# Feed-forward heads: the row of roots, the first copy of low sums and the order of the first two tiles

## The reference, cut to what matters

```
def conv_ffn(h, w_up, dw_w, dw_b, w_down):
    u = dwconv(h @ w_up, dw_w, dw_b)            # 3 taps along the tokens
    val, gate = jnp.split(u, 2, axis=-1)
    return (jax.nn.gelu(gate) * val) @ w_down
...
    h = rmsnorm(x, norm2_g[i])                  # a row of 256 inverse roots, one per token
    x = x + conv_ffn(h, ffn_w_up[i], ffn_dw_w[i], ffn_dw_b[i], ffn_w_down[i])
```

## Time and profile before

| | us |
|---|---|
| median of 3 runs (1609.86 to 1610.27) | 1610.09 |
| the profiled execution's own time | 1610.04 |
| span from its first to its last instruction | 1608.1 |
| PE busy in the span | 1573.2 (98%) |
| DVE busy | 1248.2 (78%) |
| ACT busy | 996.0 (62%) |
| DMA, mean rate over the span | 177 GB/s |

### The profile page before, as it was taken

One profiled execution on the slowest core, in us unless ns is written; L12 is line 12 of the kernel. 1 busy time (PEld: TensorE's weight loads), 2 busy tenths in 40 slices (PEclk: granted clock), 3 DMA queues, 4 the chain that ended last, 5 costly groups with the idle time before them and its releaser, 6 DMA issues.

```text
span 1608.1 us, 25361 instructions
## 1 busy us (share of the span) xinstructions
PE 1573.2 (98%) x8810; PEld 1344.2 (84%) x8810; DVE 1248.2 (78%) x1828; ACT 996.0 (62%) x1406; POOL 102.4 (6%) x110
## 2 busy tenths in 40 slices
PE   9999999999999999999999999999999999999998
PEld 9887888878878889868888898868788887878887
DVE  6756888878798887866888886456788887878887
ACT  6576665675676656666666655444666666666664
POOL 0031000000000001340000042000100000000000
PEclk9999999999999999999999999999999999999999
DMA  9434455543645554443555555524555554345553
GB/s 344 153 111 171 181 188 203 183 174 115 239 162 186 195 192 158 165 151 131 183 201 184 189 190 191 195 105 158 183 195 183 185 180 183 140 149 186 185 198 135
DMA packets 43393, 285.44 MB, mean 177 GB/s; under 512 B 5280, under 2 KB 5408, under 8 KB 10688
## 3 DMA queue, kind: packets, MB, share of 16 engines
q1 hardware_dynamic: 40592, 274.96, 47.7%
q0 software_dynamic: 2736, 9.60, 1.8%
HBM read 282.43 MB, written 1.05 MB: 176 GB/s over the span
## 4 chain that ended last, share of the span: by engine, by line
PE 80%; DVE 12%; ACT 5%; issue 3%; DMA 0%; SPq 0%; POOL 0%; DVEq 0%
PE bank L2263 21%; PE bank L2266 10%; PE bank L2162 7%; PE bank L2163 7%; PE bank L2164 7%; PE bank L2112 4%; PE bank L2113 4%; PE bank L2114 4%; DVE w_lo L1230 3%; PE bank L2059 3%; PE bank L2060 3%; PE bank L2061 3%; DVE arena L1527 2%; DVE arena L1513 1%; DVE arena L1510 1%
## 5 line engine op out<-in xcount | busy, mean ns | idle before, releaser
L2263 PE MATMUL bank<-h_both,w_hi 128*128 128x512 f32 x1760 | 554.7, 396 | 10.3 <-DVE arena L1510 6.2
L2266 PEld LDWEIGHTS bank<-h_both,w_lo 128*128 128x128 f32 x1760 | 330.6, 188 | 77.6
L1230 DVE TENSOR_TENSOR w_lo<-raw,w_hi 128x2048 fp32r<-128x2048 f32 (+3 forms) x133 | 289.9, 2180 | 104.3 <-ACT w_hi L698 103.6
L2266 PE MATMUL bank<-h_both,w_lo 128*128 128x256 f32 x1760 | 346.0, 278 | 0.0
L698 ACT ACTIVATE w_hi<-raw 128x2048 fp32r<-128x2048 f32 (+3 forms) x135 | 245.1, 1816 | 100.6 <-PE bank L2164 37.3
L2263 PEld LDWEIGHTS bank<-h_both,w_hi 128*128 128x128 f32 x1760 | 271.6, 189 | 17.6 <-issue 8.2
L1547 DVE TENSOR_TENSOR w_lo<-raw,w_hi 128x2048 fp32r<-128x2048 f32 x120 | 274.1, 2284 | 0.0
L2162 PE MATMUL bank<-w_hi,h_both 128*128 128x512 f32 x632 | 247.9, 392 | 4.2 <-DVE h_both L1541 4.2
L2163 PE MATMUL bank<-w_lo,h_both 128*128 128x512 f32 x632 | 246.2, 390 | 0.0
L2164 PE MATMUL bank<-w_hi,h_both 128*128 128x512 f32 x632 | 246.1, 389 | 0.0
L919 ACT ACTIVATE w_hi<-raw 128x2048 fp32r<-128x2048 f32 x120 | 228.4, 1904 | 0.0
(11 more groups left out here) (236 smaller groups left out, 1858.0 us busy)
## 6 DMA issues: line engine op xcount, KB each, us to landing
raw<-wstream SPq DMA_DIRECT2D x252, 1024.0 KB, 4.8
raw<-wstream SPq DMA_DIRECT2D x8, 256.0 KB, 3.9
raw<-wstream SPq DMA_DIRECT2D x4, 512.0 KB, 8.1
arena<-dilated_bias POOLq DMA_DIRECT2D x8, 256.0 KB, 4.8
arena<-conv_rows POOLq DMA_DIRECT2D x2, 1024.0 KB, 4.7
arena<-window_bias POOLq DMA_DIRECT2D x4, 512.0 KB, 6.0
raw<-wstream SPq DMA_DIRECT2D x4, 384.0 KB, 3.5
cst<-consts SPq DMA_DIRECT2D x1, 1088.0 KB, 11.9
```

Of the source, the lines that this page charges most:

```text
L1230: nc.vector.tensor_tensor(w_lo[:, s, 0:w], raw[:, s, 0:w], w_hi[:, s, 0:w].bitcast(F32), ALU.subtract)\
L2263: nc.tensor.matmul(halves(up_banks(a)[:, m, :]), w[m][0], h_both[:, kt, :, :], start=kt == 0, stop=kt == 7, skip_group_check=True)
L2266: last = nc.tensor.matmul(up_banks(a)[:, m, 0:S], w[m][1], h_hi[:, kt, :], start=False, stop=kt == 7, skip_group_check=True)
```

## The change

Four edits, all in the head of a feed-forward stage:

- PE: `root_row` stands behind the second k-tile of up(1) (kt == 1) in place of the sixth (kt == 5).
- ACT: `low_sums` of tile 0 moves ahead of the copy of the row (as `first_sums`, passed to `prenorm` as its `then`). The one-element SiLU activation, and so its table load, falls away in feed-forward stages; convolution stages keep it.
- ACT: `gelu` of tile 1 moves from ahead of `low_sums` of tile 2 to behind `split_hi` of chunk c0+5.
- DVE: `split_lo` of chunk c0+4 and `low_part` of tile 0 move ahead of `taps` of tile 1.

```
+            def first_sums(c0):
+                act.wait_ge(chunk_used, c0 + 1)
+                nc.scalar.activation(halves(up_l[:, 0, :]), up_banks(0)[:, :, S:2 * S], ACT.Copy).then_inc(up_low, 1)
...
-                low_sums(0, 0, c0 + 1)
                 centre(0, 0)
                 split_hi(c0 + 3)
                 low_sums(1, 1, c0 + 2)
                 gelu(0, 0)
                 split_hi(c0 + 4)
                 centre(1, 1)
                 high_part(0, 8, c0 + 2)
-                gelu(1, 1)
                 low_sums(2, 0, c0 + 3)
                 split_hi(c0 + 5)
+                gelu(1, 1)
                 high_part(1, 9, c0 + 2)
...
-                if name.startswith(("ffn", "conv")):
+                if name.startswith("ffn"):
+                    then = lambda: first_sums(c0)
+                if name.startswith("conv"):
                     then = lambda: tables_of(ACT.Silu)
...
                 split_lo(c0 + 3)
                 up_norm(1, 1)
                 gated_value(0, 0)
+                split_lo(c0 + 4)
+                low_part(0, 8)
                 taps(1, 1)
-                split_lo(c0 + 4)
                 gated_value(1, 1)
-                low_part(0, 8)
                 low_part(1, 9)
                 up_norm(2, 0)
                 split_lo(c0 + 5)
...
-                        if between and kt == 5:
+                        if between and kt == 1:
                             between()
```

## The result

The changed kernel takes 1597.72 us (median of four, 1597.24 to 1598.35) beside 1609.98 for the kernel before: 12.3 us less, a ratio of 0.9921 with a 95% interval of 0.9908 to 0.9933. The forecast was 1597.5.

A forecast was written before the change was run, and what follows sets the result against it. DVE's queue up to chunk c0+6 was taken to set when PE starts up(5) in each feed-forward head. First part 10.33 plus second part 2.2 gave 12.5 us off 1610.0, so 1597.5 us, range 1595.5 to 1602.5.

The forecast's parts named there:

- The bound: In each feed-forward head, a stage's gain is how much earlier up(5) starts on PE, set by DVE's queue; 2.46 us a stage.
- First part: Earlier row and first copy let DVE start its first sum sooner: 2.25 us in the first head, 2.02 in four, 10.33 total.
- The cover of 1.2 us: On ACT in the second head, both copies are done 1.2 us before DVE wants them, so their work costs nothing.
- Table load: Dropping ACT's SiLU load is worth under 1 us in five stages by the trace; some 8 with the skill page's drain.
- rival A: On ACT, a 1.28 us table load lands ahead of the first centre tap, cutting the gain to 1.2 a stage: 1604; 6 in 100.
- Second part: New order of the first two tiles on ACT and DVE brings tile 2's first sum 0.44 us earlier a stage, 2.2 in five.
- The stop that grows: PE's three earlier stops in the head go, and the fourth, at up(5), grows from 0.74 to about 1.0 us.
- The sum: Over five feed-forward heads, 10.33 + 2.2 = 12.5 us, from 1610.0 to 1597.5 us.
- The term for it in the range: For the spread of runs (0.4 us over three), the range's lower end went from 1596.0 to 1595.5.
- rival B: PE becomes the head's bound because DVE's chain shrinks more; up(5) starts at 462.83, 3.44 earlier: 1592.8; 4 in 100.
- rival D: On ACT, a late load for chunk c0+5's split holds gelu 1 and DVE's queue, one per stage per microsecond: 1616; 5 in 100.
- Rival E: The longer last stop at up(5) halves PE's clock, one up product taking 5.6 us longer: 1625; 2 in 100.

The follow-up runs named there:

- split early: Changed kernel with chunk c0+3's high part ahead of tile 0's centre tap on ACT and its low part ahead of tile 0's taps on DVE: 1591.34 us.
- first part alone: Changed kernel with the old order of the first two tiles on ACT and DVE, keeping the row, first copy and table load edits: ratio 0.9939.
- late split: Changed kernel with three useless 128 x 512 copies on ACT ahead of the split of chunk c0+5 in each head: ratio 0.9976 to the kernel before.
- pad in the queue: Changed kernel with one useless 128 x 512 product on DVE in each head, ahead of the taps of tile 2, where DVE doesn't idle: 1601.24 us.
- row first: Changed kernel with root_row behind the first k-tile of up(1) (kt == 0): median 1598.28 us.

## Why the prediction was right

**The bound.** That a stage's gain is read at up(5), and there from DVE's queue, held in every run. Kernels with first sums from 2.21 to 4.47 us behind the split, third sums from 13.95 to 15.09 behind the first, and pads, all have up(5) where that queue ends: 0.13 us behind the split of chunk c0+6 in the four later heads of each, 0.06 in the first. In the split early, with 12.65, PE takes over. But DVE's queue is not DVE's work alone. Between the first sum and the split of chunk c0+4 it runs by way of ACT: the centre tap waits for DVE's product, the taps for the centre tap, and that split for ACT's high part, which comes behind ACT's split of c0+3 and GELU's own table load (1.28). DVE was free there only about 0.1 us sooner. So the rival that ACT bounds the head did not fall in that stretch: the two engines end it within about 0.1 us of each other, and by these rows less work for DVE alone, behind its product with the row of roots, would have won nothing there. No run here took work from ACT in that stretch.

**First part.** Forecast 2.02 us in the second head, 2.25 in the first, 10.3 in all; measured 4.23 - 2.21 = 2.02, 4.47 - 2.21 = 2.26, and 10.3 in the heads of the first part alone. The cover of 1.2 us for both copies was 1.37.

**Table load.** Under 1 us forecast by the row, some 8 by the drain; 0.4 measured. The centre tap ran without a load of its own (ACT's rows 434.75 and 437.95 follow one another), so rival A fell.

**Second part.** Forecast 0.44, measured 0.46. The step from the tail of the stage (taps to low part in 3.02 us) was the right row: here it is 450.46 - 447.44 = 3.02. The wait ahead of chunk c0+4 came out as worked out, the split starting 444.90 - 436.50 = 8.40 behind the first sum. ACT had 0.31 left ahead of gelu 1, where 0.38 were forecast.

**The stop that grows.** Forecast "about 1.0", measured 1.08 of idle time. It showed as the 5.1 us of the waits.

**The sum.** 12.5 forecast, 12.6 in the heads, 12.3 in the medians, which carry a spread of a microsecond from the start of the program that the three runs before had not shown (0.4). The term for it in the range, 0.5, was too small. That the median lies only 0.2 from the forecast is therefore in part luck; that the heads lie 0.1 from it is not.

**What was off.** In rival B, PE's own limit for up(5) was put 34.11 behind up(0) (462.83 - 428.72); the early split shows 33.83. I had taken the length of down(0) and up(4), 11.28, from a stretch that begins with a restart after a stop; down(0) alone takes 5.57 there and 5.47 without a stop. And I had taken off the 0.74 of the bracket, where the stop at up(5) cost PE 0.89 (the k-tile before began at 464.68, and 466.27 - 464.68 - 0.70 = 0.89). So a shorter DVE queue was worth 1.25 a head there, not 1.05. In rival D, the price "one per stage" for each microsecond was right for up(5), and lacked the clock.

**Rival E** was put as a stop of about 1.0 us lowering the clock. It did not: in the changed kernel, and with stops of 1.4 and 1.7 us, up(5) runs on at 1.00. But the mechanism exists: stops of 1.9 to 2.1 us were followed by it in four heads of five, at 1.6 us a fall, where I had written 5.6. The Trainium skill, page "TensorE: Matmul & The Clock Gate", section "HAM oscillation — how this bites in real kernels", tells of such falls after idle gaps of PE; the late split is the run here that shows it.

Not tried: a really late load. The late split holds ACT in its place.

## What to carry to other kernels

Where an engine stops several times in a row for another, look whether only the last stop counts, as here: follow the other engine's queue to it, and price an edit by what it takes out of that queue, waits included. The waits name the second engine on the path; here that was ACT. The same instruction cost all of its time in the queue and nothing in a wait, so look for waits of the bounding engine and put work that is ready into them. Price a moved sequence from a place in the trace where the same sequence already runs back to back.

## What the runs showed of the hardware that was not expected

In the late split, stops of PE of 1.9 to 2.1 us were followed by a fall of the granted clock to the lower level in four of five heads, costing 1.6 us each. In the pad in the queue, with stops of 1.4 us in the first head and 1.7 in the others, there was none:

```profile
463.06:469.06 6.00, 6.00 (x34) 1.00 0.50 175
```

That is the stretch behind up(5) in the second head of the pad in the queue. The attention stage, where PE is busy for some 7 of 8 us and makes short stops of up to 1.0 us, has such a fall in four of the twelve profiles, costing 1.2 us. That it comes and goes between executions of one kernel is only suggested: in the row first the profiled execution, with the fall, has a mean granted clock of 0.998 and takes 1599.17, the other three 1.000 and 1598.2 to 1598.3. Together with the start of the program this would make most of the spread between runs. Of the heads the four later ones repeat to 0.04 us within each profile.
